# The last expert pair of a mixture-of-experts step: two landings for a weight run, a product split by contraction, statistics on the scalar engine

## The reference

```python
def moe(x2, w_router, b_router, w_gu, b_gu, w_down, b_down):
    ...
    gates = jax.nn.softmax(top_vals, axis=-1)
    ...
    def expert_block(args):
        tok, e = args
        xb = x_pad[tok]
        gu = xb @ w_gu[e] + b_gu[e]
        gate, up = gu[:, :D_FF], gu[:, D_FF:]
        gate = jnp.minimum(gate, SWIGLU_LIMIT)
        up = jnp.clip(up, -SWIGLU_LIMIT, SWIGLU_LIMIT)
        h = (up + 1.0) * gate * jax.nn.sigmoid(SWIGLU_ALPHA * gate)
        return h @ w_down[e] + b_down[e]
    ...
y = layer_norm(DEEPNORM_ALPHA * h + f, ln2_g, ln2_b)
```

## Time and profile before

| | |
|---|---|
| median of 3 runs | 1130.44 us (1130.36 to 1130.7) |
| time of the profiled execution | 1133.25 us |
| its span in the trace | 1131.2 us |
| PE busy | 1084.0 us, 96% of the span |
| DVE, ACT, POOL busy | 314.1, 180.7, 89.4 us |
| HBM read | 431.78 MB, 385 GB/s over the span |

### The profile page before, as it was taken

One profiled execution on the slowest core, in us unless ns is written; L12 is line 12 of the kernel. 1 busy time (PEld: TensorE's weight loads), 2 busy tenths in 40 slices (PEclk: granted clock), 3 DMA queues, 4 the chain that ended last, 5 costly groups with the idle time before them and its releaser, 6 DMA issues.

```text
span 1131.2 us, 13406 instructions
## 1 busy us (share of the span) xinstructions
PE 1084.0 (96%) x5494; PEld 534.8 (47%) x5494; DVE 314.1 (28%) x574; ACT 180.7 (16%) x310; POOL 89.4 (8%) x48
## 2 busy tenths in 40 slices
PE   8999999999999999999999999989898989898994
PEld 5889945535444343434343434343434343343431
DVE  3584955321212213030303120303030302112114
ACT  3242101111111111111111201111111111111101
POOL 4675400000000000000000000000000000000002
PEclk9999999899999999999999999999999999999998
DMA  9963387899999999999999999999999999999993
GB/s 353 335 214 112 127 320 268 347 399 408 424 426 428 426 428 426 427 430 426 427 428 429 430 427 428 429 431 427 428 427 430 429 427 428 429 429 426 428 427 135
DMA packets 52640, 436.23 MB, mean 386 GB/s; under 512 B 5952, under 2 KB 15936, under 8 KB 25888
## 3 DMA queue, kind: packets, MB, share of 16 engines
q1 hardware_dynamic: 46080, 428.67, 91.5%
q10 hardware_dynamic: 6528, 7.09, 1.8%
HBM read 431.78 MB, written 3.97 MB: 385 GB/s over the span
## 4 chain that ended last, share of the span: by engine, by line
PE 65%; DMA 25%; DVE 1%; POOL 0%; issue 0%; ACT 0%; DVEq 0%; SPq 0%; POOLq 0%
PE bank L906 25%; DMA ring<-w_down 21%; PE bank L932 17%; PE bank L842 8%; PE bank L582 4%; DMA old_rooms<-w_down 3%; PE bank L712 2%; DMA xy<-x_tok 1%; PE bank L958 1%; PE bank L887 1%; PE bank L960 1%; PE bank L767 1%; PE bank L915 1%; PE bank L737 0%; PE bank L851 0%; PE bank L854 0%
## 5 line engine op out<-in xcount | busy, mean ns | idle before, releaser
L906 PE MATMUL bank<-ring,xg 128*64 128x512 f32 x1536 | 345.2, 595 | 7.2 <-DMA ring<-w_gu 7.1
L906 PEld LDWEIGHTS bank<-ring,xg 128*64 128x64 f32 x1536 | 105.4, 136 | 209.4 <-issue 187.6
L932 PE MATMUL bank<-ring,act_t 128*64 128x512 f32 x672 | 150.7, 594 | 7.0 <-DMA ring<-w_down 7.0
L906 PE MATMUL bank<-old_rooms,xg 128*64 128x512 f32 x496 | 112.4, 595 | 5.0 <-DMA old_rooms<-w_gu 5.0
L1558 DVE SCALAR_TENSOR_TENSOR oo_lo<-oo_raw,gate_s,oo_hi 128x512 fp32r<-128x512 f32 x32 | 24.0, 751 | 311.3 <-ACT oo_hi L1133 311.3
L1585 DVE TENSOR_SCALAR gate_c<-bank 128x512 f32<-128x512 f32 x32 | 22.1, 692 | 264.2 <-PE bank L906 264.2
L842 PEld LDWEIGHTS bank<-onehot,hid 128*128 128x128 f32 x720 | 85.9, 196 | 12.2 <-issue 12.2
L932 PEld LDWEIGHTS bank<-ring,act_t 128*64 128x64 f32 x672 | 46.2, 136 | 90.7 <-issue 78.3
L842 PE MATMUL bank<-onehot,hid 128*128 128x128 f32 x720 | 88.8, 283 | 0.0
L1571 DVE TENSOR_TENSOR xy<-xy,bank 128x512 f32<-128x512 f32 x84 | 52.7, 682 | 107.7 <-PE bank L960 107.7
L1210 POOL TENSOR_TENSOR rstd<-veps,minus_half 128x1 f32<-128x1 f32 x6 | 3.3, 546 | 980.1 <-DVE veps L1379 980.1
(11 more groups left out here) (211 smaller groups left out, 869.8 us busy)
## 6 DMA issues: line engine op xcount, KB each, us to landing
ring<-w_gu SPq DMA_DIRECT2D x90, 2048.0 KB, 30.5
ring<-w_down SPq DMA_DIRECT2D x41, 2048.0 KB, 33.0
old_rooms<-w_gu SPq DMA_DIRECT2D x30, 2048.0 KB, 30.6
old_rooms<-w_down SPq DMA_DIRECT2D x13, 2048.0 KB, 32.9
ring<-w_in SPq DMA_DIRECT2D x13, 1024.0 KB, 14.5
ring<-w_gu SPq DMA_DIRECT2D x12, 1024.0 KB, 5.7
old_rooms<-w_down SPq DMA_DIRECT2D x6, 1024.0 KB, 10.1
over_q<-w_down SPq DMA_DIRECT2D x3, 2048.0 KB, 17.3
```

Source lines behind the costliest of these rows:

```text
L906: mm = pe.matmul(bank[2 * a + n][64 * hf:64 * hf + 64, :], xg[:, c, 64 * a:64 * a + 64], w[:, col:col + 512], start=False, stop=(c == KC - 1))
L932: mm = pe.matmul(bank[b][64 * hf:64 * hf + 64, :], act_t[:, a, c % 4, 64 * (c // 4):64 * (c // 4) + 64], w[:, c % run, hf * 512:(hf + 1) * ...
```

## The change

Four things change.

1. In odd pairs the last run (w_down of expert b, its second half of the contraction) is issued as two DMAs of 1 MB. The first raises `last_low_full`, the second the room's `slot_full`. `down` waits for the first before c = 4 and for the second before c = 6.
2. In the last pair `down` of expert b becomes `down_last`. The two column groups now take neighbouring parts of the contraction (c and c + 1) of the same half of the outputs. Half 0 collects in bank 5 and half 1 in bank 4; partitions 0 to 63 and 64 to 127 each hold half of the contraction's sum. `gt_last` and `gate_last` hold expert b's slots twice, so the combining product adds the two parts. ACT makes `oo_hi` straight from PSUM and DVE `oo_lo` too; the copies to `oo_raw` are gone.
3. Expert a's outputs no longer share the combining product with b's. `combine_first` adds them with twelve products of their own (contraction 64), placed before c = 4 of `down_last`.
4. The statistics of token tile 2 move from DVE to ACT (two sums, a mean, two sums of squares), and DVE turns them into a variance in `last_variance`. POOL now makes all three inverse roots ahead of its work on tile 0.

```diff
@@ pair_pieces, on SP
-                    expert_run(j, ea, eb, rooms(g % WIDE, units)).then_inc(slot_full[g % WIDE], 16)
+                    if odd and j == PAIR_PIECES - DN_UNITS:
+                        k = (DN_PIECES - DN_UNITS) * 256
+                        rows = w_down[bass.ds(eb, 1), k:k + 128 * DN_RUN, :].rearrange("e (p k) n -> p e (k n)", p=128)
+                        for n, landed in enumerate((last_low_full, slot_full[g % WIDE])):
+                            sp.dma_start(rooms(g % WIDE, units)[:, n * PW:(n + 1) * PW].unsqueeze(1),
+                                         rows[:, :, n * PW:(n + 1) * PW]).then_inc(landed, 16)
+                    else:
+                        expert_run(j, ea, eb, rooms(g % WIDE, units)).then_inc(slot_full[g % WIDE], 16)
@@ on PE
+            def down_last(turn, between):
+                for hf in range(2):
+                    pe.matmul(bank[last_down_banks[hf]][0:64, :], sel_down[:, 1, :],
+                              biasp[:, 2 * FF + hf * 512:2 * FF + (hf + 1) * 512], start=True, stop=False)
+                for c in range(0, KC, 2):
+                    if c in between:
+                        between[c]()
...
+                    if c == KC - 2:
+                        run_landed(PAIR_PIECES - DN_UNITS, DN_UNITS, turn, True)
+                    for hf in range(2):
+                        for g in range(2):
+                            mm = pe.matmul(bank[last_down_banks[hf]][64 * g:64 * g + 64, :],
+                                           act_t[:, 1, (c + g) % 4, 64 * (c // 4):64 * (c // 4) + 64],
+                                           w[:, (c + g) % DN_RUN, hf * 512:(hf + 1) * 512],
+                                           start=(c == 0 and g == 1), stop=(c == KC - 2))
+                        if c == KC - 2 and hf == 0:
+                            mm.then_inc(half_down, 1)
+                    mm.then_inc(piece_used, 1)
+            def combine_first(p):
+                pe.wait_ge(gt_ready, 2 * p + 2)
+                pe.wait_ge(oo_hi_ready, 2 * p + 2)
+                pe.wait_ge(oo_lo_ready, 2 * p + 2)
+                for hf in range(2):
+                    for t in range(NT):
+                        for part in (oo_hi, first_lo):
+                            pe.matmul(bank[last_banks[2 * t + hf]][:, :], gt[0:64, t * 128:(t + 1) * 128],
+                                      part[0:64, hf, :], start=False, stop=False)
@@ pair, on PE
-                down(1, turn, odd, {})
+                if last:
+                    pe.wait_ge(out_ready, 4 * p + 2)
+                    down_last(turn, {4: lambda: combine_first(p)})
+                else:
+                    down(1, turn, odd, {})
@@ on ACT
+            def last_high_outputs(p):
+                act.wait_ge(piece_used, PAIR_PIECES * p + MIX_PIECES + PAIR_PIECES - 1)
+                for n in range(2):
+                    act.dma_start(lnp[:, n, :], ln2[n:n + 1, :].to_broadcast([128, D])).then_inc(ln2_in, 16)
+                act.wait_ge(gt_last_ready, 2)
+                for hf in range(2):
+                    if hf == 0:
+                        act.wait_ge(half_down, 1)
+                    else:
+                        act.wait_ge(piece_used, PAIR_PIECES * p + MIX_PIECES + PAIR_PIECES)
+                    act.activation(oo_hi[:, hf, :], bank[last_down_banks[hf]][:, :], ACT.Copy, scale=gate_last[:, 0:1])\
+                        .then_inc(oo_hi_ready, 1)
@@ the end, on ACT
+            for n in range(2):
+                act.wait_ge(comb_mm, 6 * last_pair + NT * (n + 1))
+                act.activation((sig, gate_c)[n][:, :], bank[last_banks[2 * (NT - 1) + n]][:, :], ACT.Identity, scale=-1.0 / D,
+                               accum_out=sums[:, n:n + 1]).then_inc(row_sum, 1)
+            act.wait_ge(row_sum, 2)
+            act.activation(sums[:, 2:3], sums[:, 0:1], ACT.Identity, bias=sums[:, 1:2]).then_inc(row_sum, 1)
+            act.wait_ge(row_sum, 3)
+            for n in range(2):
+                act.activation(act_h[:, n, :], bank[last_banks[2 * (NT - 1) + n]][:, :], ACT.Square, bias=sums[:, 2:3],
+                               accum_out=sums[:, 3 + n:4 + n]).then_inc(row_square, 1)
             act.wait_ge(y_shift, 1)
@@ the end, on POOL
-            row_rstd(NT)
+            for t in range(NT):
+                row_rstd(NT + t)
...
-                row_rstd(NT + 1 + n)
@@ the end, on DVE
+            def last_variance():
+                dve.wait_ge(row_square, 2)
+                link(dve.tensor_tensor(sums[:, 5:6], sums[:, 3:4], sums[:, 4:5], ALU.add))
+                dve.tensor_scalar(veps[:, NT - 1:NT], sums[:, 5:6], 1.0 / D, EPS, ALU.mult, ALU.add).then_inc(ln_var, 1)
...
             centre(1)
-            sums_stats(2)
+            last_variance()
             finish(1)
```

More of the change, by code:

```diff
@@ L233, in build @@
         up_c = sb("up_c", [128, 512])
+        with ExitStack() as early:
+            gt_last = sb("gt_last", [128, T], F32R, early)
         onehot = sb("onehot", [128, NT, 128])
         sig = sb("sig", [128, 512])
+        with ExitStack() as early:
+            first_lo = sb("first_lo", [128, 2, 512], F32R, early)
         xg = sb("xg", [128, KC, 128])
@@ L241, in build @@
         gate_s = sb("gate_s", [128, 1])
-        kept = (KC + 2 * H) * T + 3 * NT * DR - (4 * D + 3 * T + 2 * SLOTS + 3 * 512 - NT * 128 + 2 * NT + 1) - 2 * PW
+        gate_last = sb("gate_last", [128, 1])
+        sums = sb("sums", [128, 6])
+        kept = (KC + 2 * H) * T + 3 * NT * DR - (4 * D + 3 * T + 2 * SLOTS + 3 * 512 - NT * 128 + 2 * NT + 8) - 2 * PW
         with ExitStack() as gap:
@@ L865, in landed, with run_room @@
                 return room(g % WIDE)
+            def run_room(j, units, odd):
+                return rooms(pair_fill(j, odd) % WIDE, units)
             def run_landed(j, units, turn, odd):
@@ L1148, in pair @@
                     if last and a:
-                        act.wait_ge(piece_used, PAIR_PIECES * p + MIX_PIECES + PAIR_PIECES - 1)
-                        for n in range(2):
-                            act.dma_start(lnp[:, n, :], ln2[n:n + 1, :].to_broadcast([128, D])).then_inc(ln2_in, 16)
+                        last_high_outputs(p)
+                        continue
                     act.wait_ge(piece_used, PAIR_PIECES * p + MIX_PIECES + 2 * GU_PIECES + DN_PIECES * (a + 1))
                     for hf in range(2):
-                        if not (last and a and hf):
-                            act.copy(oo_raw[64 * a:64 * a + 64, hf, :],
-                                     bank[down_banks[a]][64 * hf:64 * hf + 64, :]).then_inc(out_ready, 1)
+                        act.copy(oo_raw[64 * a:64 * a + 64, hf, :],
+                                 bank[down_banks[a]][64 * hf:64 * hf + 64, :]).then_inc(out_ready, 1)
                         if a:
-                            high_outputs(p, hf, last)
+                            high_outputs(p, hf)
+                    if last:
+                        for hf in range(2):
+                            first_high_outputs(p, hf)
                     if a == (1 if first else 0) and not last:
@@ L1545, in slots_of, with first_low_outputs, last_low_outputs, low_outputs @@
                 gates_of(n)
-            def low_outputs(p, last=False):
+            def first_low_outputs(p):
                 dve.wait_ge(gt_ready, 2 * p + 2)
                 for hf in range(2):
[L1551 to L1556, removed]
+                    dve.wait_ge(oo_hi_ready, 2 * p + hf + 1)
+                    dve.scalar_tensor_tensor(first_lo[0:64, hf, :], oo_raw[0:64, hf, :], gate_s[0:64, 0:1],
+                                             oo_hi[0:64, hf, :].bitcast(F32), ALU.mult, ALU.subtract).then_inc(oo_lo_ready, 1)
+            def last_low_outputs(p):
+                dve.wait_ge(gt_last_ready, 3)
+                for hf in range(2):
+                    dve.wait_ge(oo_hi_ready, 2 * p + hf + 3)
+                    dve.scalar_tensor_tensor(oo_lo[:, hf, :], bank[last_down_banks[hf]][:, :], gate_last[:, 0:1],
+                                             oo_hi[:, hf, :].bitcast(F32), ALU.mult, ALU.subtract).then_inc(oo_lo_ready, 1)
+            def low_outputs(p):
+                dve.wait_ge(gt_ready, 2 * p + 2)
+                for hf in range(2):
+                    dve.wait_ge(out_ready, 4 * p + 3 + hf)
                     dve.wait_ge(oo_hi_ready, 2 * p + hf + 1)
@@ L1607, in pair @@
                 if last:
[L1609 to L1611 removed]
+                    first_low_outputs(p)
+                    last_low_outputs(p)
                     return
@@ L1652, in finish @@
                                              lnp[:, 1, o], ALU.mult, ALU.add).then_inc(y_done, 1)
-            for t in range(NT):
+            for t in range(NT - 1):
                 half_stats(t, 0)
```

63 lines of the change are left out of this document (47 added, 16 removed).

## The result

The change makes the kernel slower by 1.6 us: 1132.31 us median (1130.43 to 1134.52, 20 runs) against 1130.70 (1128.92 to 1131.71, 20 runs), a ratio of 1.0015 with an interval of 1.0009 to 1.0021. The middle is within the 0.2% that the prediction called no change, and 0.1 us from the predicted 1132.4. So close a hit is partly luck: the prediction added 1.9 us to a median of 1130.44, and the change added 1.6 us to one of 1130.70.

What follows compares the result with a forecast made beforehand. The weight stream was taken to pace the expert loop and POOL to decide the end. DMA +0.3 and tail +1.6 make +1.9 us, added to the 1130.44 median: 1132.4 us, range 1130.8 to 1134.0.

Steps and rivals of the forecast that it cites:

- DMA, +0.3 us: Weight stream: five split runs before the last w_gu wait cost 0.3 us, between nothing and 0.95.
- The upper bound of 0.19 a split: DMA queue: 2 MB takes 5.09 instead of 4.90 us at 412 against 428 GB/s; five splits 0.95 at most.
- PE before the last run, +2.9: PE in the last pair: bias products 0.2 and twelve combining products 3.1 start the last run 2.9 us later.
- From down to the statistics, +1.6: Tail after the last down product: DVE's first statistic starts at 1118.3 instead of 1116.72, +1.6 us.
- DVE's end, as before: Norm on DVE: `finish(1)` starts at 1123.45 instead of 1123.21 and ends at about 1127.6, as before.
- ACT in time for `last_variance`: Norm on ACT: its tile 2 sums are ready for `last_variance` at 1122.97, in time by 0.5 us.
- POOL, +2.56 at its first multiplication and +1.6 at its last operation: Norm on POOL: third root delays tile 0's first multiplication by 2.56 us; four operations end 1.6 us later.
- Sum: Whole kernel: +0.3 (DMA) and +1.6 (tail) make +1.9 us, for 1132.4 us, +0.17%.
- the hidden products: Rival, PE in the last pair: the twelve products cost 1.6 instead of 3.1 us, 1130.9, no change; chance 0.09.
- the loop gain: Rival, expert loop: PE's waits shrink by 0.5 to 1 us in each of six, 1127 to 1130; chance 0.09.
- The long statistics: Rival, ACT: statistics longer than plain rows; at 0.5 us more each the end is 1 us later, 1133.4; chance 0.08.
- The costly split: Rival, DMA queue: splits cost the stream more; 1133.0 at 0.19 us each, 1137 at 1 us; chance 0.08.

Runs made afterwards that it cites:

- the run with one landing: The changed kernel with the last w_down run of the odd pairs in one DMA again, with one wait: 1132.59 us, ratio 1.0014.
- the run with the order alone: Changed kernel, norm reordered: ACT scales tile 0 before its sums of squares, DVE's variance after `finish(1)`, POOL's third root between tile 0's halves: 1132.06 us, ratio 1.0013.

## Why the prediction was right

All numbers are from the anchor on, as differences to the kernel before.

- **DMA, +0.3 us.** At the measured 0.08 us a split, five splits are 0.4. In the change itself this term can't be seen: the medians leave 0.1 us for it, within their noise, and the run with one landing is no faster. The upper bound of 0.19 a split, from 412 GB/s in an early stretch, was over twice too high. The reason given, a queue less full there, does not fit: the DMA share of that stretch is 1.02.
- **PE before the last run, +2.9.** Measured +2.85. The twelve products took 1109.27 - 1106.31 = 2.96 us, they began 0.25 later than the last run could have before (the bias pair), and 0.36 of waiting went away. The step held because the earlier trace rows showed that PE waited only 0.2 us for the last landing: there was nothing for the products to hide behind. Leaving them out moved `oo_hi` by 3.1.
- **From down to the statistics, +1.6.** Measured +1.36 (1114.37 - 1086.88 = 27.49 against 1116.72 - 1090.59 = 26.13). `oo_hi` starts within 0.1 of its place; the second `oo_lo` ended a little sooner than I had it.
- **DVE's end, as before.** Measured 0.4 earlier (36.55 against 36.98). It decides nothing.
- **ACT in time for `last_variance`.** It was: its second sum of squares is read at 1118.58 and DVE starts the variance at 1119.12, when `centre` is done. The margin is the 0.5 us foreseen.
- **POOL, +2.56 at its first multiplication and +1.6 at its last operation.** Measured +2.35 and +1.57. The chain ran as foreseen: third root, and behind it four operations in series. That the root holds POOL is shown by moving it. That the end agrees to 0.03 is luck: the series started 0.2 sooner than forecast and took 5.17 us instead of 5.0.
- **Sum.** +1.9 predicted, of which +1.6 behind the anchor; there +1.51 was measured, and +1.61 in the medians.

Of the rivals, the hidden products and the loop gain are out, by the run without the products and by the loop's equal busy time of PE (56.61 and 56.62 of 60 us) and equal rate of 428 GB/s. The long statistics are out as well: an activation with a sum output took 0.60 us and its read 0.19, together near the plain 0.77. The costly split is real in its mechanism and too small to decide.

What the prediction did not look for is that part of the old tail was open to gain: SP's fixed store order. It became costly only with the change, which let DVE finish 1.8 us before POOL.

## What to carry to other kernels

Before work is split so that it can start earlier on partial data, read how long the engine really waits for that data, and what the split adds: here 0.4 us were to be won from the landing and 0.6 by finishing one half earlier, and the split forced twelve products of 3 us onto the same engine. When work moves off a loaded engine, follow the in-order queues of all that are left: the third root and the store order, each one line, held operations of a tile they don't serve. And compare two kernels from an anchor that both traces share, since the early part moved by 3.7 us between executions and hid a difference of 1.5.

## What was not expected of the hardware

A two-operand DVE operation on single columns in SBUF took 0.73 us, and 0.72 in the run with the order alone, while POOL worked on a 128x512 addition, and ended with it within 0.01 us both times; alone it took 0.15. The Trainium skill, "SBUF — State Buffer", section "SBUF: two separate sides", states that a DVE operation with two SBUF inputs and a POOL operation that reads SBUF take a shared port pair in turn, each for a whole instruction. The traces agree with that: ACT's single-column operations at the same place kept their 0.29 us, and early in the changed kernel the other side waits: a POOL operation of 2.40 us alone took 4.17 (76.62 to 80.79) where a DVE addition with two SBUF inputs ran until 78.54.

Two DMAs of 1 MB in a full queue cost 0.08 us more than one of 2 MB, on busy DMA engines. An activation with a sum output shows as two instructions, the second one `ACTIVATION_READ_ACCUMULATOR` of 0.19 to 0.21 us.
